# Who sums the gathered expert rows, and which way the first work item's rows take

## The reference

```python
logits = (h @ router_w).astype(jnp.float32)
top_val, top_idx = lax.top_k(logits, TOP_K)
gates = jax.nn.softmax(top_val, axis=-1)
combine = jnp.sum(jax.nn.one_hot(top_idx, N_EXPERTS) * gates[..., None], axis=-2)
for e in range(N_EXPERTS):
    y = y + combine[..., e:e + 1] * swiglu(h, w_gate[e], w_up[e], w_down[e])
```

## Time and profile before

| what | value |
|---|---|
| median of 3 runs | 1792.99 us (1792.06 to 1793.48) |
| the profiled execution's own time | 1793.41 us |
| its span, first to last instruction | 1791.7 us |
| TensorE busy | 1697.6 us, 95% |
| VectorE busy | 1300.9 us, 73% |
| ScalarE busy | 1050.0 us, 59% |
| GpSimd busy | 125.4 us, 7% |
| chain that ended last, by engine | TensorE 85%, VectorE 7%, ScalarE 4%, DMA 1% |
| DMA | 491.67 MB, 274 GB/s over the span |

### The profile page before, as it was taken

How to read it: one execution, slowest core, us unless ns; L and a number is a source line. 1 busy time by engine, 2 the same in 40 slices (tenths; PEclk the granted TensorE clock), 3 DMA queues, 4 the chain that set the end, 5 groups by cost and what they waited for, 6 DMA issues and landing times.

```text
span 1791.7 us, 24418 instructions
## 1 busy us (share of the span) xinstructions
PE 1697.6 (95%) x9352; PEld 1453.0 (81%) x9352; DVE 1300.9 (73%) x1096; ACT 1050.0 (59%) x916; POOL 125.4 (7%) x107
## 2 busy tenths in 40 slices
PE   5996989999999998979999999999999999999889
PEld 4974989999999987868878878788788788787766
DVE  4865355544964466458888888888888888888997
ACT  4424244434343275437787777777877877878655
POOL 2014000000001000010000000000000000000750
PEclk9997699999998899969999999999999999999999
DMA  7515049855557332739999999999999999999984
GB/s 257 182 61 167 1 154 363 270 177 189 176 189 257 124 104 80 270 123 380 338 375 392 364 366 379 357 382 368 351 396 363 358 391 350 374 375 352 370 302 150
DMA packets 237366, 491.67 MB, mean 274 GB/s; under 512 B 8733, under 2 KB 66337, under 8 KB 237040
## 3 DMA queue, kind: packets, MB, share of 16 engines
q1 hardware_dynamic: 227800, 456.56, 71.2%
q0 software_dynamic: 9504, 34.24, 5.8%
HBM read 463.29 MB, written 27.95 MB: 274 GB/s over the span
## 4 chain that ended last, share of the span: by engine, by line
PE 85%; DVE 7%; ACT 4%; issue 3%; DMA 1%; ACTq 0%; SPq 0%; DVEq 0%
PE bank L668 25%; PE bank L669 24%; PE bank L670 24%; DVE WL L1610 2%; PE bank L979 2%; PE bank L810 1%; PE bank L916 1%; PE bank L1173 1%; DVE WL L1586 1%; ACT WH L1505 1%; DMA ring<-in_w_in_even 1%; PE bank L1137 1%; PE bank L967 1%; ACT WH L1233 1%; ACT L1505 1%
## 5 line engine op out<-in xcount | busy, mean ns | idle before, releaser
L1610 DVE TENSOR_TENSOR WL<-moe_MORE,WH 128x2048 fp32r<-128x2048 f32 x192 | 450.9, 2353 | 85.0 <-ACT WH L1505 83.5
L1505 ACT ACTIVATE WH<-moe_MORE 128x2048 fp32r<-128x2048 f32 x192 | 367.5, 1918 | 165.0 <-PE bank L670 164.9
L1610 DVE TENSOR_TENSOR WL<-ring,WH 128x2048 fp32r<-128x2048 f32 x144 | 338.4, 2355 | 57.5 <-ACT WH L1505 57.4
L668 PE MATMUL bank<-WH,moe_XEH 128*128 128x512 f32 x896 | 361.3, 403 | 9.5 <-DVE WL L1610 6.5
L670 PE MATMUL bank<-WH,moe_XEL 128*128 128x512 f32 x896 | 355.0, 396 | 0.0
L669 PE MATMUL bank<-WL,moe_XEH 128*128 128x512 f32 x896 | 354.9, 396 | 0.0
L1505 ACT ACTIVATE WH<-ring 128x2048 fp32r<-128x2048 f32 x144 | 275.9, 1918 | 95.5 <-PE bank L670 95.5
L668 PE MATMUL bank<-HH,WH 128*128 128x264 f32 x960 | 282.9, 295 | 17.8 <-DVE HL L1604 12.0
L1586 DVE TENSOR_TENSOR WL<-ring,WH 128x2048 fp32r<-128x2048 f32 x80 | 181.1, 2263 | 137.7 <-ACT WH L1233 137.5
L669 PE MATMUL bank<-HL,WH 128*128 128x264 f32 x960 | 277.4, 289 | 0.0
L670 PE MATMUL bank<-HH,WL 128*128 128x264 f32 x960 | 276.8, 288 | 0.0
(11 more groups left out here) (337 smaller groups left out, 1919.6 us busy)
## 6 DMA issues: line engine op xcount, KB each, us to landing
moe_MORE<-in_moe_w_gate SPq DMA_DIRECT2D x72, 1024.0 KB, 6.6
moe_MORE<-in_moe_w_up SPq DMA_DIRECT2D x72, 1024.0 KB, 6.9
ring<-in_moe_w_down SPq DMA_DIRECT2D x64, 1024.0 KB, 6.8
moe_MORE<-in_moe_w_down SPq DMA_DIRECT2D x48, 1024.0 KB, 6.4
ring<-in_moe_w_gate SPq DMA_DIRECT2D x40, 1024.0 KB, 6.0
ring<-in_moe_w_up SPq DMA_DIRECT2D x40, 1024.0 KB, 6.8
ring<-in_w_in_odd SPq DMA_DIRECT2D x24, 1024.0 KB, 5.4
ring<-in_ffn_w_gate SPq DMA_DIRECT2D x11, 1024.0 KB, 8.6
```

Of the source, the lines that this page charges most:

```text
L668: mm(out, lh, rh, start=start, stop=False)
L1505: func(WH[:, q % WRING, :], chunk(q), ACT.Copy).then_inc(s_hi, 1)
L1610: V.tensor_tensor(WL[:, q % WRING, :], chunk(q), full(WH[:, q % WRING, :]), ALU.subtract)\
```

## The change

GpSimd's twelve arithmetic operations behind the gathers are taken out. VectorE does the same sums with twelve operations of its own, each a product with a gate and a sum (`scalar_tensor_tensor`), in two halves of 512 columns. They stand behind the loop over the items, where VectorE's only work had been the copy GT and the six additions of the last item's result.

The first item's rows go through XS and XG like those of all others. The table OH and its matmuls are gone; SP waits for the scatters behind chunk `X_FIRST` = 8 of the first item and loads the rows there, and `turn_in(0)` transposes them ahead of the loop. The transposes of OL and the copy GT move ahead of the loop too, before `turn_in(0)`. Two counters that had two writers (`s_cm`, `s_lg`) are split in two each (`s_cv`, `s_lf`).

```diff
+        X_FIRST = MRING + 1
@@ sync, load_expert
+                    if isinstance(it, int) and c == X_FIRST:
+                        rows_in(0, (s_rows, 16 * 2 * NT))
                     if c == X_NEXT:
-                        if isinstance(it, int):
-                            sp.wait_ge(s_rows, 16 * 2 * NT)
                         rows_in(it + 1, (s_xtp, it + 1))
@@ gpsimd, behind the gathers
-            pool.wait_ge(s_xr, 2 * NT)
-            for t in range(NT):
-                rows = slice(0, TOK[t])
-                y0, y1 = YO[rows, t, :], SPARE[t][rows, :]
-                pool.wait_ge(s_gy[t], 32)
-                for c, y in enumerate((y0, y1)):
-                    nc.gpsimd.tensor_tensor(y, y, GE[rows, t, 2 + c:3 + c].to_broadcast([TOK[t], D]), ALU.mult)\
-                        .then_inc(s_pre, 1)
-                pool.wait_ge(s_pre, 4 * t + 2)
-                nc.gpsimd.tensor_tensor(y0, y0, y1, ALU.add).then_inc(s_pre, 1)
-                pool.wait_ge(s_pre, 4 * t + 3)
-                nc.gpsimd.tensor_tensor(y0, y0, XR[t][rows, :], ALU.add).then_inc(s_pre, 1)
@@ tensor
-            pe.wait_ge(s_oh, 1)
-            pe.wait_ge(s_hx, 2 * NT)
-            for k in range(DK):
-                for t in range(NT):
-                    last = mm(PB[2 if k < 4 else 7][:, (k % 4) * P:(k % 4 + 1) * P],
-                              HX[0:TOK[t], t, k * P:(k + 1) * P], OH[0:TOK[t], t, :],
-                              start=(t == 0), stop=(t == NT - 1))
-            last.then_inc(s_xtp, 1)
             def turn_in(it):
-                pe.wait_ge(s_xl, it * 16)
+                pe.wait_ge(s_xl, it * 16 + 16)
...
+            pe.wait_ge(s_hx, 2 * NT)
+            pe.wait_ge(s_last, 1)
+            for t in range(NT):
+                last = turn(PB[7][:, t * P:t * P + TOK[t]], OL[0:TOK[t], t, :], ident[0:TOK[t], 0:TOK[t]])
+            last.then_inc(s_turn, 1)
+            turn_in(0)
             with pe.Fori(0, n_items) as it:
...
-            pe.wait_ge(s_last, 1)
-            for t in range(NT):
-                last = turn(PB[7][:, t * P:t * P + TOK[t]], OL[0:TOK[t], t, :], ident[0:TOK[t], 0:TOK[t]])
-            last.then_inc(s_turn, 1)
@@ scalar
-            copy_in(0, (2, 7))
+            copy_in(0)
@@ vector
-            slots = PB[3][:, 0:P]
-            for t in range(NT):
-                last = V.tensor_scalar(OH[:, t, :], slots, DF[:, t:t + 1], None, ALU.is_equal)
-            link(last)
-            for t in range(NT):
-                last = V.scalar_tensor_tensor(out=OH[:, t, :], in0=slots, scalar=DF[:, NT + t:NT + t + 1],
-                                              in1=OH[:, t, :], op0=ALU.is_equal, op1=ALU.add)
-            last.then_inc(s_oh, 1)
...
-            low_in(0, (2, 7))
+            dve.wait_ge(s_turn, 2 * DK + CT + 1)
+            V.tensor_copy(GT[:, :], PB[7][:, 0:T]).then_inc(s_last, 1)
+            low_in(0)
@@ vector, behind the loop
-            dve.wait_ge(s_turn, 2 * DK + CT + 1)
-            V.tensor_copy(GT[:, :], PB[7][:, 0:T]).then_inc(s_last, 1)
+            dve.wait_ge(s_xr, 2 * NT)
             for half in range(2):
                 cols = slice(half * 512, (half + 1) * 512)
                 for t in range(NT):
+                    rows = slice(0, TOK[t])
+                    dve.wait_ge(s_gy[t], 32)
+                    last = V.scalar_tensor_tensor(out=YO[rows, t, cols], in0=YO[rows, t, cols],
+                                                  scalar=GE[rows, t, 2:3], in1=XR[t][rows, cols],
+                                                  op0=ALU.mult, op1=ALU.add)
+                link(last)
+                for t in range(NT):
+                    rows = slice(0, TOK[t])
+                    last = V.scalar_tensor_tensor(out=YO[rows, t, cols], in0=SPARE[t][rows, cols],
+                                                  scalar=GE[rows, t, 3:4], in1=YO[rows, t, cols],
+                                                  op0=ALU.mult, op1=ALU.add)
+                link(last)
+                for t in range(NT):
+                    rows = slice(0, TOK[t])
                     dve.wait_ge(s_turn, 2 * DK + CT + 2 + NT * half + t)
-                    dve.wait_ge(s_pre, 4 * t + 4)
-                    y = YO[0:TOK[t], t, cols]
-                    V.tensor_tensor(y, PB[back_bank(half, t)][0:TOK[t], :], y, ALU.add).then_inc(s_yo, 1)
+                    V.tensor_tensor(YO[rows, t, cols], PB[back_bank(half, t)][rows, :], YO[rows, t, cols], ALU.add)\
+                        .then_inc(s_yo, 1)
```

More of the change, by code:

```diff
@@ L261, in build @@
         EI = region("moe", "EI", TI_N + 2)
-        OH = SI[:, :, :].rearrange("p a n -> p (a n)")[:, 0:NT * P].rearrange("p (t n) -> p t n", n=P)
         YO = region("moe", "YO", NT, D, at=2 * H * T + 2 * RV)
@@ L291, in build @@
         s_ag = sem("s_ag"); s_sig = sem("s_sig"); s_u = sem("s_u"); s_ut = sem("s_ut"); s_uo = sem("s_uo")
-        s_dg = sem("s_dg"); s_cg = sem("s_cg"); s_conv = sem("s_conv"); s_cm = sem("s_cm"); s_cd = sem("s_cd"); s_cq = sem("s_cq")
+        s_dg = sem("s_dg"); s_cg = sem("s_cg"); s_conv = sem("s_conv"); s_cm = sem("s_cm"); s_cd = sem("s_cd"); s_cq = sem("s_cq"); s_cv = sem("s_cv")
         s_crt = sem("s_crt"); s_cn = sem("s_cn"); s_mixc = sem("s_mixc")
@@ L313, in build @@
         s_on = sem("s_on"); s_g = sem("s_g"); s_gs = sem("s_gs"); s_y = sem("s_y"); s_yh = sem("s_yh"); s_yl = sem("s_yl")
-        s_lfe = sem("s_lfe"); s_lg = sem("s_lg"); s_ht2 = sem("s_ht2")
-        s_oh = sem("s_oh"); s_hx = sem("s_hx"); s_dest = sem("s_dest"); s_rows = sem("s_rows")
-        s_sel = sem("s_sel"); s_pre = sem("s_pre"); s_items = sem("s_items")
+        s_lf = sem("s_lf"); s_lfe = sem("s_lfe"); s_lg = sem("s_lg"); s_ht2 = sem("s_ht2")
+        s_hx = sem("s_hx"); s_dest = sem("s_dest"); s_rows = sem("s_rows")
+        s_sel = sem("s_sel"); s_items = sem("s_items")
         s_xl = sem("s_xl"); s_xtp = sem("s_xtp"); s_xeh = sem("s_xeh"); s_xel = sem("s_xel"); s_mm = sem("s_mm")
@@ L895, in _ @@
                 last = mm(PB[2][:, 0:T], const_("mean_ch"), CQ[:, c, :], start=(c == 0), stop=(c == CT - 1))
-            last.then_inc(s_cm, 1)
+            last.then_inc(s_cv, 1)
             pe.wait_ge(s_kq, NS)
@@ L1112, in router @@
                 if half == 1:
-                    last.then_inc(s_lg, 1)
+                    last.then_inc(s_lf, 1)
             pe.wait_ge(s_xt, DK * 3 + 4)
@@ L1341, in _ @@
                 func(A[:, part], A[:, part], ACT.Exp).then_inc(s_exp, 1)
-            act.wait_ge(s_cm, 2)
+            act.wait_ge(s_cv, 1)
             func(RS[:, 0, :], PB[2][:, 0:T], ACT.Sqrt, bias=eps).then_inc(s_crt, 1)
@@ L1529, in _, with copy_in @@
             pads = act.value_load(EII[0:1, TI_N + 1:TI_N + 2], min_val=0, max_val=16 * (MAXI - E))
-            def copy_in(it, banks=(0, 1)):
+            def copy_in(it):
                 act.wait_ge(s_xtp, it + 1)
                 for i in range(2):
-                    func(XEH[:, 4 * i:4 * i + 4, :], PB[banks[i]][:, :].rearrange("p (k n) -> p k n", n=P), ACT.Copy)\
+                    func(XEH[:, 4 * i:4 * i + 4, :], PB[i][:, :].rearrange("p (k n) -> p k n", n=P), ACT.Copy)\
                         .then_inc(s_xeh, 1)
-            copy_in(0, (2, 7))
+            copy_in(0)
             with act.Fori(0, n_items) as it:
@@ L1900, in _ @@
             low_moe(0, 1)
-            dve.wait_ge(s_lg, 1)
+            dve.wait_ge(s_lf, 1)
             V.tensor_copy(LF[0:E, :], PB[3][0:E, 0:T]).then_inc(s_lfe, 1)
@@ L1904, in _ @@
             V.tensor_tensor(SM[:, 0, :], SS[:, 0, :], SS[:, 1, :], ALU.add).then_inc(s_ms, 1)
-            dve.wait_ge(s_lg, 2)
+            dve.wait_ge(s_lg, 1)
             V.tensor_copy(LG[:, 0:2, :], PB[7][:, P:P + 2 * E].rearrange("p (t e) -> p t e", e=E))
@@ L1934, in _ @@
             rows_hx(0)
-            dve.wait_ge(s_lg, 3)
+            dve.wait_ge(s_lg, 2)
             rank = PB[7][:, 0:NT * E].rearrange("p (t e) -> p t e", e=E)
@@ L1978, in _, with low_in @@
             n_items = dve.value_load(EII[0:1, TI_N:TI_N + 1], min_val=E, max_val=MAXI)
-            def low_in(it, banks=(0, 1)):
+            def low_in(it):
                 for i in range(2):
                     dve.wait_ge(s_xeh, it * 2 + i + 1)
-                    V.tensor_tensor(XEL[:, 4 * i:4 * i + 4, :], PB[banks[i]][:, :].rearrange("p (k n) -> p k n", n=P),
+                    V.tensor_tensor(XEL[:, 4 * i:4 * i + 4, :], PB[i][:, :].rearrange("p (k n) -> p k n", n=P),
                                     full(XEH[:, 4 * i:4 * i + 4, :]), ALU.subtract).then_inc(s_xel, 1)
```

## The result

The changed kernel takes 1776.78 us (median of 4 runs, 1776.33 to 1777.22), the one before 1793.24 us: a ratio of 0.990, with a 95% interval of 0.9882 to 0.9918. The profiled execution took 1777.22 us, with a span of 1775.5 us.

The account below looks back on a forecast made before the run. TensorE was taken to set the items' pace, held up in the last by VectorE's splits beside GpSimd's arithmetic. -15.6 + 3.1 - 0.1 - 1.0 = -13.6 from 1793.41 gave 1779.8, median 1779.4 us; range 1776.8 to 1784.0.

Parts of the forecast that it names:

- -15.6: Last item: without GpSimd's twelve operations splits fall from 4.00 to 2.29 us and the item takes 122.02 us, -15.6 us.
- the margin of 3 us for the weights: Last item: a weight chunk beside the gathers lands at 1690.4, ScalarE wants it at 1693.5, 3 us to spare.
- 4.00 us: Last item: average time of VectorE's weight splits while GpSimd computes, against 2.29 us while it only issues gathers.
- +3.1: Tail: the second half's six sums on VectorE delay the last addition from 1788.75 to 1791.9, +3.1 us.
- -0.1: Tail: with OL's transposes and copy GT ahead of the loop, the last matmuls wait for ScalarE's first copy, -0.1 us.
- -1.0 us: First item's rows: scatters, load and transposes end at 784.7 instead of 785.73, -1.0 us, from -2.9 to +3.0.
- The low end of the term: First item's rows, best case -2.9 us: scatter landed at 778.5, load 3.4, transposes 0.9.
- The estimate by the Trainium skill: First item's rows: 2.0 us fixed plus bytes at 436 GB/s gives 783.6, making the forecast sum 1.1 us lower.
- The range's low end: Whole kernel: 1776.8 us, lower bound of the 8-in-10 range, allowing for a shorter scatter.
- the way round DRAM: Rival on the first item's rows: late scatter and loaded-queue load cost +3.0 instead of -1.0, 1783.4 us; 15 in 100.
- the weights did not bound the item: Rival on the last item: TensorE waits 5.9 us for weights because of the gathers' traffic, 1785.3 us; 10 in 100.
- the slow splits were GpSimd's doing: Rival on the last item: gathered rows' landing or code slows splits, nothing of 15.6 recovered, 1795.0 us; 3 in 100.

Follow-up runs that it names:

- run c: Changed kernel plus twelve idle GpSimd additions in the fifth item, without gathers: that item 139.45 us instead of 122.02; ratio 1.0024 to the kernel before.
- runs changed and b: The changed kernel, and the changed kernel with the sums given back to GpSimd and the old additions: ratios 0.990 and 0.999 to the kernel before.
- run d: Changed kernel with X_FIRST one larger, so SP issues the tenth weight chunk ahead of its wait for the scatters: ratio 0.9946 to the kernel before.
- run h: Changed kernel with VectorE's third split moved from beside the scatters to behind the copy GT: ratio 0.9918 to the kernel before.
- run a: Kernel before with only the sums moved from GpSimd to VectorE, copy GT still behind the loop: ratio 0.9941 to the kernel before.

## Why the prediction was right, and where it was not

The last item: -15.6 forecast, -15.63 measured, and run c shows the cause by itself. The reading that carried it was that the length of one item is the number of its neighbours; the margin of 3 us for the weights was enough. One reading was of a part: 4.00 us is the mean of seven splits in that window, and four more took 4.63 there; the sum did not use it.

The tail: +3.1 and -0.1 forecast, +3.3 (12.73 against 9.41, runs changed and b) and -0.3 measured. Together +3.0 both times: the two misses of 0.2 us cancel, which is luck.

The step that failed is the price of the first item's rows, "-1.0 us": the mechanism held and the term was too small, -2.64. Counted from the first scatter, the forecast had 784.7 - 767.10 = 17.6 us and the trace has 15.99. Most of it is the last scatter: I took 2.4 to 3.4 us from GpSimd's release to landing, the low end from the first scatter, which carries 128 rows where the last carries 8, the high end from scatters behind each other's traffic. With only 8 rows and no load beside it, it took 1.67 us until the load began: the six scatters ended on GpSimd at 766.45 + 9.06 = 775.51, and the load began at 777.18. The load took 3.2 us and not 3.6. The issue of all six took 9.06 us and not 9.36: the masks that left VectorE did shift it, since VectorE's split came earlier and met the fifth scatter instead of the sixth. The transposes took 1.98 us and not 1.75. The low end of the term had a slip too: 776.46 + 2.4 is 778.9 and not 778.5, which makes it -2.6 and not -2.9. The estimate by the Trainium skill (DMA: Bandwidth & Descriptors, section "Anatomy of one DMA") was 783.6 for the same point, 16.5 us behind the first scatter, and so was nearer than my rows. The section gives its price for transfers that GpSimd issues, as it does the scatters; the load is SP's, and that it took the 3.2 us of this price is shown here by the trace alone. Beside a 1 MB load the price does not hold: the scatter's 32 KB took 7.6 us in the earlier trace rows and 4.7 us in run d.

Two smaller parts were not in the sum: the first item's own 0.32 us, in which the granted clock rose 4.4 us behind its first matmul instead of 5.2, and 0.65 us ahead of the whole stage. In the thirteen traces this second part moves by 10 us with the same work ahead of it, so 0.65 us can't be told from the differences between runs; that part of the miss is chance. -1.6, -0.3 and -0.65 are the 2.6 us by which the forecast missed. The range's low end, 2.6 us below the forecast, had room for the first rows' term near its bound, but not for that, the first item's 0.3 us and a difference between runs together.

Of the rivals, the way round DRAM gains time and costs none (-2.64 us); the weights did not bound the item (120.25 us, and no wait for a weight load); the slow splits were GpSimd's doing (run c).

## What to carry to other kernels

An engine with 7% busy time can cost the bottleneck more than its own work is worth: look at the duration of the same instruction beside it and away from it. Before work is moved off such an engine to the end of another's queue, look for room in that queue earlier, in pieces shorter than the slack in front of each consumer. And a small transfer that decides a start is priced by what is beside it in the queue: take it from a row of the same size in an empty queue if the change empties it.

## What was not expected of the hardware

GpSimd's copies (one SBUF input) slow a split from 2.29 to between 2.87 and 2.99 us, its additions to between 3.9 and 4.4 us. The effect goes both ways: a split beside it stretches GpSimd's issue of an indirect DMA from 0.88 to 2.70 us (run h against the changed kernel). And a wait of 1.97 us in front of six matmuls was followed by a granted clock of 0.73 on average, and the first three of their results came 1.7 to 2 times as far apart (run a).
